# Rows of the first two experts built by one-hot matmuls from the rows in SBUF, in place of the first gather

## What is computed

```python
def grouped_moe(h, w_router, b_router, w_gate, w_up, w_down):
    t = h.reshape(-1, D)
    s = jax.nn.sigmoid((t @ w_router).astype(jnp.float32))
    ...
    hid = jax.nn.silu(jnp.einsum('td,edf->tef', t, w_gate)) * jnp.einsum('td,edf->tef', t, w_up)
    hid = hid * gates.astype(hid.dtype)[:, :, None]
    out = jnp.einsum('tef,efd->td', hid, w_down)
```

## Time and profile before

| | |
|---|---|
| median of three runs | 1125.43 us |
| span of the profiled execution, first to last instruction | 1121.9 us |
| PE busy | 982.3 us, 88% |
| DVE, ACT, POOL busy | 404.9, 157.1, 123.3 us |
| moved by DMA | 328.59 MB, mean 293 GB/s |

### The profile page before, as it was taken

How to read it: one execution, slowest core, us unless ns; L and a number is a source line. 1 busy time by engine, 2 the same in 40 slices (tenths; PEclk the granted TensorE clock), 3 DMA queues, 4 the chain that set the end, 5 groups by cost and what they waited for, 6 DMA issues and landing times. The chain is left out here.

```text
span 1121.9 us, 12453 instructions
## 1 busy us (share of the span) xinstructions
PE 982.3 (88%) x4812; PEld 467.2 (42%) x4812; DVE 404.9 (36%) x902; ACT 157.1 (14%) x364; POOL 123.3 (11%) x188
## 2 busy tenths in 40 slices
PE   4799999997898989988799979999678997889886
PEld 2555545454333333333266544554523333333332
DVE  0189855245211110111435994533521111011206
ACT  1101233220000000000130014422000000000010
POOL 1001200511000000000221020060200000000010
PEclk9899889997999999988799997999579999999988
DMA  9928973368999996999950475225965999999932
GB/s 339 383 95 310 302 298 108 124 219 355 424 420 425 425 367 272 422 427 421 360 220 24 150 270 223 76 92 185 362 234 220 415 426 425 423 424 422 420 134 75
DMA packets 64570, 328.59 MB, mean 293 GB/s; under 512 B 7448, under 2 KB 10184, under 8 KB 48084
## 3 DMA queue, kind: packets, MB, share of 16 engines
q1 hardware_dynamic: 44224, 277.89, 61.6%
q0 software_dynamic: 9072, 27.89, 6.8%
q10 hardware_dynamic: 11172, 21.42, 5.8%
HBM read 305.88 MB, written 21.30 MB: 292 GB/s over the span
## 5 line engine op out<-in xcount | busy, mean ns | idle before, releaser
L1782 PE MATMUL ps<-big 128*64 128x512 f32 x1024 | 244.6, 630 | 27.6 <-issue 11.9
L1798 PE MATMUL ps<-big,scr 128*64 128x512 f32 x624 | 156.3, 644 | 5.6 <-DVE scr L1428 4.3
L1477 PE MATMUL ps<-big 128*128 128x384 f32 (+2 forms) x448 | 147.9, 492 | 5.1 <-ACT big L786 5.1
L1782 PEld LDWEIGHTS ps<-big 128*64 128x64 f32 x1024 | 78.5, 144 | 173.1 <-issue 159.5
L1124 DVE SCALAR_TENSOR_TENSOR scr<-scr,convw 128x384 f32<-128x384 f32 x240 | 134.1, 613 | 2.3
L1441 DVE TENSOR_TENSOR scr<-ps,scr 128x256 f32<-128x256 f32 x32 | 13.6, 424 | 278.2 <-ACT scr L953 278.1
L1477 PEld LDWEIGHTS ps<-big 128*128 128x128 f32 x448 | 86.0, 193 | 64.7 <-issue 24.8
L1798 PEld LDWEIGHTS ps<-big,scr 128*64 128x64 f32 x624 | 50.6, 148 | 97.9 <-issue 96.9
L1698 PE MATMUL ps<-big 128*128 128x512 f32 x192 | 84.4, 594 | 1.4 <-ACT big L826 1.4
L1493 PE MATMUL ps<-big,cs_rep 128*32 128x256 f32 x640 | 49.5, 466 | 14.4 <-DMA big<-in_w_mod_dram 14.4
L953 ACT ACTIVATE scr<-ps 128x256 f32<-128x256 f32 x32 | 12.3, 383 | 325.2 <-PE ps L1782 325.2
(11 more groups left out here) (231 smaller groups left out, 842.5 us busy)
## 6 DMA issues: line engine op xcount, KB each, us to landing
big<-in_w_gate_dram SPq DMA_DIRECT2D x32, 2048.0 KB, 18.4
big<-in_w_up_dram SPq DMA_DIRECT2D x32, 2048.0 KB, 22.8
big<-in_w_down_dram SPq DMA_DIRECT2D x32, 2048.0 KB, 18.9
big<-in_w_mod_dram SPq DMA_DIRECT2D x23, 2048.0 KB, 15.3
big<-in_w_in_dram SPq DMA_DIRECT2D x6, 2048.0 KB, 23.5
expert_rows<-scr ACTq DMA_DIRECT2D x68, 128.0 KB, 8.5
big<-in_w_out_dram SPq DMA_DIRECT2D x4, 2048.0 KB, 19.8
expert_rows<-x ACTq DMA_DIRECT2D x1, 7168.0 KB, 42.6
```

Of the source, the lines that this page charges most:

```text
L1477: mm = pe.matmul(out, stationary(k), moving(k), start=(k == 0), stop=(k == n - 1))
L1782: mm = pe.matmul(ps[b * TT:(b + 1) * TT, bank, :].rearrange("p (m n) -> p m n", m=2), tokens(k), w[:, :, k, b * HF:(b + 1) * HF], start=(k ...
L1798: mm = pe.matmul(ps[b * TT:(b + 1) * TT, bank, :], src[:, k % 2 * P + k // 2 * TT:k % 2 * P + (k // 2 + 1) * TT], w[:, k, b * SEG:(b + 1) ...
```

## The change

The first gather goes. DVE makes, from the positions of experts 0 and 1, one-hot marks `first_mark` (three tiles of 128 tokens by 128 places); PE multiplies them with `h` in SBUF (two sums of three products, 128 columns by 512), which gives the 128 rows of block 0 in PSUM banks 0 and 1. ACT copies the first half to `ov_x`, DVE the second; PE transposes them, ahead of the matmuls for `slot_tok`; ACT takes one half of the transposes and DVE the other. POOL starts with the gathers of blocks 1 and 2, and from then on is a block further ahead. `h` is read until the second sum is done, so slot 7 is lent back only then (`first_rows_ps`), under an entry "rows" of its own in `place()`, after "norm", which now frees slot 6 alone. This moves loads to other slots in both layers.

```diff
@@ -73,7 +73,7 @@
         at = next((n for n, s in enumerate(free) if s < limit), None)
         while at is None:
             done = order.pop(0)
-            free.extend((SLOTS, SLOTS + 1) if done == "norm" else (slot[done],))
+            free.append({"norm": SLOTS, "rows": SLOTS + 1}[done] if done in ("norm", "rows") else slot[done])
             at = next((n for n, s in enumerate(free) if s < limit), None)
         slot[item] = free.pop(at)
         count[slot[item]] += 1
@@ -93,16 +93,18 @@
                 order += held
             if item == ("out", l, 1):
                 order.append("norm")
+            if item == ("v", l, 5, 1):
+                order.append("rows")
         order += [("g", l, 0), ("u", l, 0)]
         for e in range(1, E):
             order += [("d", l, e - 1), ("g", l, e), ("u", l, e)]
         order.append(("d", l, E - 1))
         for item in experts:
             take(item, MOE_SLOTS)
-        ends.append(count[SLOTS])
+        ends.append((count[SLOTS], count[SLOTS + 1]))
         while order:
             done = order.pop(0)
-            if done != "norm":
+            if done not in ("norm", "rows"):
                 free.append(slot[done])
         free = [s for s in free if s < SLOTS]
     return slot, use, ends
@@ -335,6 +337,8 @@
         col_mark = scr[:, TILES * 2 * P:TILES * 2 * (P + E // 2 * NT)].rearrange("p (n c) -> p n c", c=E // 2 * NT)
         ov_mid = cut(D)
         ov_xsT, ov_ybuf = ov_mid[:, 0:KD * TT], ov_mid[:, KD * TT:D]
+        first_mark = ov_mid[:, 0:TILES * P].rearrange("p (t n) -> p t n", t=TILES)
+        first_pos = scr[:, 6560:6560 + 2 * TILES].rearrange("p (t n) -> p t n", n=2)
         rt = yflat
         sel_all = rt[:, 528:576]
         last_mark = scr[:, 6144:6144 + TILES * P].rearrange("p (t n) -> p t n", t=TILES)
@@ -375,6 +379,8 @@
         first_half = sem("first_half"); cache_st = sem("cache_st"); h2_st = sem("h2_st")
         filled_st = sem("filled_st")
         iota_ready = sem("iota_ready"); marks_ready = sem("marks_ready")
+        first_marks = sem("first_marks"); first_rows_ps = sem("first_rows_ps"); first_rows = sem("first_rows")
+        first_xT = sem("first_xT")
         y_st = [sem(f"y_st{b}") for b in range(2)]
         gathered = [sem(f"gathered{b}") for b in range(2)]
         picked = [sem(f"picked{t}") for t in range(TILES)]
@@ -482,12 +488,12 @@
                 def slot_free(n):
 
                     s = slot_of(n)
-                    if s >= SLOTS and uses(n) - 1 == (BORROWED[l - 1] if l else 0):
+                    if s >= SLOTS and uses(n) - 1 == (BORROWED[l - 1][s - SLOTS] if l else 0):
                         if s == SLOTS:
                             sp.wait_ge(h_ready, l * 3 + 3)
                         else:
                             sp.wait_ge(h2_st, (l + 1) * (TILES * 16))
-                            sp.wait_ge(logit_ps, l * 3 + 3)
+                            sp.wait_ge(first_rows_ps, l * 2 + 2)
                     elif past(uses(n) - 1):
                         sp.wait_ge(slot_used[s], uses(n) - 1)
                     return s
@@ -565,7 +571,7 @@
                         norm_rstd(0, l, t)
 
                 if l:
-                    pool.wait_ge(slot_used[SLOTS], BORROWED[l - 1])
+                    pool.wait_ge(slot_used[SLOTS], BORROWED[l - 1][0])
                 lane_in(pool, rowB, b_mod[l:l + 1, 3 * D:4 * D], rowB_in)
                 pool.dma_start(rowS, b_mod[l:l + 1, 4 * D:5 * D].broadcast_to([2, D])).then_inc(rowB_in, 16)
 
@@ -650,8 +656,9 @@
                         .then_inc(gathered[i % 2], 16)
 
                 pool.wait_ge(h2_st, (l + 1) * (TILES * 16))
-                gather(0)
                 gather(1)
+                gather(2)
+                pool.wait_ge(xT_ps, l * (E // 2) + 1)
 
                 pool.wait_ge(mod_taken, taken_at(l, 5))
                 lane_out(pool, mod_dram[:, 5 * D:6 * D], rowG, modG_st)
@@ -677,9 +684,9 @@
                             for t in range(2, NT):
                                 run(t)
                         pool.reg_add(ov_at, ov_at, 0)
-                    if e % 2 and e + 3 < E:
-                        pool.wait_ge(xT_ps, l * (E // 2) + e // 2 + 1)
-                        gather(e // 2 + 2)
+                    if e % 2 and e + 5 < E:
+                        pool.wait_ge(xT_ps, l * (E // 2) + e // 2 + 2)
+                        gather(e // 2 + 3)
 
 
                 stored = pool.snap(ov_count)
@@ -891,6 +898,10 @@
                     if t:
                         h2_tile(t - 1)
                 h2_tile(2)
+                act.wait_ge(first_rows_ps, l * 2 + 1)
+                a.copy(ov_x[:, 0:SEG], ps[:, 0, :]).then_inc(first_rows, 1)
+                act.wait_ge(xT_ps, l * (E // 2) + 1)
+                a.copy(hT[0][:, 0:4, :].rearrange("p k n -> p (k n)"), ps[:, XT, :]).then_inc(first_xT, 1)
                 act.wait_ge(rows_ready, l + 1)
 
                 def take_y(k):
@@ -1308,6 +1319,14 @@
 
                 step.link(v.tensor_scalar(code_base, slot_base, float(SEG) / CAP, None, ALU.mult))
                 dve.wait_ge(pos_ps, l + 1)
+                if l == 0:
+                    dve.wait_ge(iota_ready, 1)
+                step.link(v.tensor_copy(first_pos, by_tile(ps[:, 5, 0:NE])[:, :, 0:2]))
+                for t in range(TILES):
+                    for e in range(2):
+                        ins = v.tensor_scalar(first_mark[:, t, e * TT:(e + 1) * TT], iota[:, 0:TT], first_pos[:, t, e:e + 1],
+                                              by_tile(sel)[:, t, e:e + 1], ALU.is_equal, ALU.mult)
+                ins.then_inc(first_marks, 1)
                 step.link(v.tensor_tensor(by_tile(pm), by_tile(ps[:, 5, 0:NE]),
                                           code_base.unsqueeze(1).broadcast_to([P, TILES, E]), ALU.add))
                 step.link(v.tensor_tensor(pm, pm, sel, ALU.mult))
@@ -1322,15 +1341,17 @@
                 step.mark(v.tensor_scalar(code[:, 1, :], code[:, 0, :], 10, None, ALU.logical_shift_right))
                 step.link(v.tensor_scalar(code[:, 2, :], code[:, 0, :], 6, 7, ALU.logical_shift_right, ALU.bitwise_and))
                 step.link(v.scalar_tensor_tensor(col_n, code[:, 1, :], float(NT), code[:, 2, :], ALU.mult, ALU.add))
-                if l == 0:
-                    dve.wait_ge(iota_ready, 1)
                 for n in range(TILES * 2):
                     t = n // 2
                     v.tensor_scalar(row_mark[:, n, :], iota[:, :], row_n[:, n:n + 1], None, ALU.is_equal)
                     v.tensor_scalar(col_mark[:, n, :], iota[:, 0:E // 2 * NT], col_n[:, n:n + 1], tok_id[:, t:t + 1],
                                     ALU.is_equal, ALU.mult).then_inc(marks_ready, 1)
                 v.tensor_copy(count[0:1, 0:E], ps[0:1, 5, NE:NE + E]).then_inc(pos_ready, 1)
+                dve.wait_ge(first_rows_ps, l * 2 + 2)
+                v.tensor_copy(ov_x[:, SEG:D], ps[:, 1, :]).then_inc(first_rows, 1)
                 mod_take(l, 5)
+                dve.wait_ge(xT_ps, l * (E // 2) + 1)
+                v.tensor_copy(hT[0][:, 4:8, :].rearrange("p k n -> p (k n)"), ps[:, XT + 1, :]).then_inc(xsT_ready, 1)
                 dve.wait_ge(slots_ps, l + 1)
                 v.tensor_copy(slot_tok[:, :], ps[:, 6, 0:E // 2 * NT]).then_inc(slots_ready, 1)
                 if l + 1 < LAYERS:
@@ -1448,7 +1469,6 @@
                     if e < E - 1:
                         overflow(dve, n, run, ov_at)
 
-                take_xT(0)
                 if l + 1 < LAYERS:
                     mod_take(l + 1, 1)
                 for mark, first, pos, w in ((last_mark, 0, pos15, w15), (mark14, 0, pos14, w14), (mark15b, TT, pos15, w15)):
@@ -1748,8 +1768,16 @@
                 accumulate(ps[:, 5, TILES * E:(TILES + 1) * E], lambda k: ones,
                            lambda k: sel_all[:, k * E:(k + 1) * E], TILES).then_inc(pos_ps, 1)
                 vector(l, 5, 6, KD)
+                pe.wait_ge(first_marks, l + 1)
+                for b in range(2):
+                    accumulate(ps[:, b, :], lambda t: first_mark[:, t, :], lambda t: h[:, t, b * SEG:(b + 1) * SEG], TILES)\
+                        .then_inc(first_rows_ps, 1)
                 if l + 1 < LAYERS:
                     vector(l + 1, 0, 0, 4)
+                pe.wait_ge(first_rows, l * 2 + 2)
+                for m in range(KD):
+                    mm = pe.transpose(ps[:, XT + m // 4, m % 4 * P:(m % 4 + 1) * P], ov_x[:, m::KD], ident)
+                mm.then_inc(xT_ps, 1)
                 for n in range(TILES * 2):
                     pe.wait_ge(marks_ready, l * TILES * 2 + n + 1)
                     mm = pe.matmul(ps[:, 6, 0:E // 2 * NT], row_mark[:, n, :], col_mark[:, n, :],
@@ -1844,6 +1872,8 @@
 
                     if j == 0:
                         pe.wait_ge(xsT_ready, l * (E // 2) + i + 1)
+                    if e == 0:
+                        pe.wait_ge(first_xT, l + 1)
                     if past(g0):
```

(5 more changed lines are left out.)

## The result

The changed kernel took 1133.12 us (median of four, 1131.8 to 1135.66) where the kernel before took 1124.13 us (four, 1115.67 to 1126.11). The ratio is 1.0114, with a 95% interval of 1.0073 to 1.0155. It is slower by 1.1%, under two per cent but clear of the noise, and the prediction, 1124 us with a range to 1131, was wrong. The profiled execution has a device time of 1132.47 us.

A forecast was written before the change was run, and what follows sets the result against it. The prediction saw PE waiting for the first gather, with DVE's routing arithmetic next in line. Layer 0 would lose 4.1 us and layer 1 gain 5.5, -1.4 on 1125.43, giving 1124 us, range 1115 to 1131.

The forecast's parts named there:

- Price zero, cover 10 us or so: Layer 1, POOL's gathers of blocks 1 and 2 starting 7 us later: no cost, about 10 us to spare.
- Jumps over the second pass: Rival, chance 0.13: PE's 3.7 us stalls at ends of experts come or go; one each way, 1120 to 1128 us.
- Layer 0's routing: Positions to expert 0: begins 1.4 us later, at 287.5, plus 2.7 for the low clock; loss of 4.1 us.
- the ends of 5.3 and 10.5: Six one-hot products on PE: 5.3 us at 2.4 GHz, 10.5 at 1.2; 7.0 taken.
- Layer 1's first piece: Layer 1, routing through expert 0: DVE's product after expert 0 comes at 826.1 instead of 831.59, gain 5.5 us.
- the good end, 7.6: Layer 1's gain if the products take 5.3 us and the rest runs at full clock: 7.6 us.
- The clock stays up: Rival, chance 0.15: products take 5.3 us in both layers, both good ends, 1117 us.
- Shifts at full value: Both layers: a shift of expert 0 passes through the later experts to the end, counted in full.
- The lent slot: Layer 0, load u1 waits for the products, from 263.42 to 271.0: cost zero, 7.6 us if uncovered.
- The sum: Layer 0's loss of 4.1 less layer 1's gain of 5.5: -1.4 on 1125.43, giving 1124 us.
- The three signs that I named for being wrong: Layer 0's expert 0 before 284, products taking 10 us, or PE waiting for weights early in layer 0.

The follow-up runs named there:

- late marks: One-hot rows in layer 1 only, against the kernel before, with gates and marks behind expert 0's product and mark transposes behind expert 1's gate and up: 1120.78 us, ratio 1.0003.
- early gather: The kernel with one-hot rows in layer 1 only and gates and marks later, plus POOL issuing expert 1's second-pass gather before the gate rows: 1115.29 us, 0.9958 of before.
- before_products: Kernel before plus six unread 128x512 products (twelve recorded instructions) on x and the identity in layer 0's routing: 1124.3 us, one profiled execution, no ratio.
- after_both: Changed kernel with POOL's old gather order and v(1,1) copied ahead of VectorE's arithmetic in layer 0: 1124.08 us, ratio 1.0054 to the kernel before.

## Why the prediction was wrong, point by point

- **The step that failed: POOL.** "Price zero, cover 10 us or so" was worked out for the gathers of blocks, in layer 1. For layer 0 POOL had no price and no row at all. The change makes POOL wait for a later event in front of each block's gather, and POOL's queue holds the gathers of second passes behind it. In layer 0 that moved one from 351.60 to 386.05, the transfer then took 16.5 us from issue to landing, and PE needed the rows at 398.3. Price: 6.6 us here, and 12.7 us where the wait stood alone.
- **Left out of the sum, and mis-sized as a rival: the stalls.** "Jumps over the second pass" named the right place, and that the lack is one of instructions the traces bear out. It had taken one stall each way as an even trade. The kernel after looks like a trade: the two of 7.4 us in all, which had stood late in layer 0, are gone, and two of 5.5 us stand early. But it is none. With POOL's order put back the late ones are there as well (3.88 and 3.76 us), and so they are with the products alone (4.10 and 3.67). The early ones were added. What took the place of the late ones in the kernel after are waits for weights, 7.7 us for 1.8; the waits of PE in the experts of layer 0:

```profile
PE ps L1840 <- issue: 5.5, 2, 2.9
PE ps L1810 <- DMA big<-in_w_up_dram: 7.7, 3, 3.3
```

The stretch from there to layer 1's positions took 378.5 us, and 379.7 with POOL's order back and all four stalls, against 380.2 before; so the late stalls cost or give little, as if the loads set the pace there, which is argued from this alone. Early in the layer PE sets the pace, and the new stalls cost about their length, 5.0 us. The groups behind them ran low (8.78 and 8.68 us for 7.09), but one of the two, expert 2's, had done so before.
- **Layer 0's routing: right.** Forecast a loss of 4.1 us, measured 5.2. Expert 0 at 288.34 for 287.5, released 1.1 us behind the copy at 286.80, at a low clock for 9.71 us for 10.07. The products took 8.48 for the 7.0 that I chose, inside the ends of 5.3 and 10.5. The cause was the one named: VectorE's arithmetic, pushed back by the products. The run with the copy moved ahead shows it: expert 0 then began 6.6 us sooner behind the positions.
- **Layer 1's first piece: right in kind, too small in size.** Forecast 5.5, measured 8.5: products 5.42 for 7.0, and expert 0 at full clock, 7.09 for 10.07, which I had seen only as the good end, 7.6. The rival "The clock stays up" was thus true of layer 1 and not of layer 0. What I missed is that this end is followed by a wait for VectorE and a low clock in expert 1, so that 1.9 comes back at once.
- **Shifts at full value: right, nearly.** The second pass of expert 7 came 16.4 us later than before, and layer 1's positions still 14.7; PE had no wait for a weight in layer 0 before 498 us. In layer 1 the window before the end of expert 1's second pass still shows the DMA engines empty, share 0.00:

```profile
863.00:867.00 4.00, 1.99 (x10) 0.88 (x10) 1.27 (x3) 0.38 (x1) 0.00 (x0) 1.00 0.00 0
```

- **The lent slot: right.** u1 was issued at 272.14 for 263.42, 271.0 forecast, and no one waited for it.

```profile
272.14 0.33 SPq L505 DMA_DIRECT2D big<-in_w_up_dram  x1
```

- **The sum.** With 4.1 and 5.5 replaced by what was measured, 5.2 and 8.5 - 1.9, the sum is still -1.4. The 10.2 us between it and the +8.8 of the traces are, up to rounding, the two prices that it lacked, 6.6 and 5.0, less 1.3 us over the rest of the table. The three signs that I named for being wrong did not appear: I had looked for the error at the products and not in the queues around them.

## What to carry to other kernels

When a change makes one engine's wait stronger, list everything behind that wait in its queue, in every layer, and ask when each item was issued before: here a gather for a rare second pass paid for it. When a wait is removed, walk down the queue of the engine that had been working under its cover, and then of the next; in layer 1 the gain reached the end only with two reorderings, on VectorE and on GpSimd. And work that looks cheap on the busiest engine may bring stalls of a few us far behind it; the same instructions with nobody reading them, in the kernel before, show that quickly. Where a stall has no releaser, look among the DMA queues for the instructions' own.

## What the runs showed of the hardware

- Six float32 products of 128x512 behind a gap of 0.8 us took 8.48 us in one layer and 5.42 in the other, and at the latter place 8.46 (late marks) and 6.90 (early gather) in two other kernels: the same work behind the same gap, between the two ends of its price. In layer 0 of `before_products`, with no gap in front of them, they took 5.42, and in layer 0 of `after_both`, behind the same gap, 5.42 too:

```profile
263.51 5.42 PE L1477 MATMUL ps<-x,table_sb 128*128 128x512 f32 x12
```

- The same gather of 512 KB took 9.50 us from issue to landing in layer 1's routing and 16.5 us amid the experts of layer 0. The share of the DMA engines does not tell the two apart, it was 0.94 and 1.01. Three more of them in the experts of layer 0 (issued at 313.07, 341.14 and 342.46) took 11.7, 11.1 and 13.9 us, and one at 407.50, where the share was 0.58 over 7 us, took 5.7. Both slow ones, 13.9 and 16.5, were issued 1.3 us behind another gather. The cover that a gather needs has to be read from the stretch in which it will run.

```profile
808.00:818.00 10.00, 0.37 (x2) 0.40 (x3) 6.85 (x49) 0.00 (x0) 4.13 (x6) 0.50 0.94 391
384.00:403.00 19.00, 13.28 (x65) 4.85 (x64) 2.89 (x6) 1.05 (x3) 1.88 (x2) 1.00 1.01 407
```

- PE's wait of 4.28 us cost more than its length, because the work behind it ran partly at the low clock: 9.57 us, for 7.09 at the full one (mean granted clock 0.74). The down projection behind that, 5.22 us, had been as slow before the change (5.35), so it is not part of the price.
- PE's stalls of over 2 us at the idle matmuls, for which no row names a releaser, were waits for instructions: a block of 16 KB landed in each of the 59, 1.2 to 1.6 us before PE went on. A few more matmuls in one place brought two of them some 40 and 70 us further on, and shifts of the whole program by 32, 228 and 256 instructions did not.
